# First modulation weights by columns in four parts, units 0 and 1 side by side, small vectors on the sync queue

## The reference, cut to what matters

```python
mod = (jax.nn.silu(c) @ w_ada + b_ada)[:, None, :]        # 6 x 1024 columns
sh1, sc1, gt1, sh2, sc2, gt2 = jnp.split(mod, N_MOD, axis=-1)
h = _rmsnorm(x, norm1_g) * (1.0 + sc1) + sh1
proj = h @ w_in                                            # the "units": 128 columns each
...                                                        # RWKV-7 and GLA branches, gates, merge
h2 = _rmsnorm(x, norm2_g) * (1.0 + sc2) + sh2
x = x + gt2 * _hier_moe(h2, router_group, router_expert, expert_w_gate, expert_w_up, expert_w_down)
```

## Time and profile before

| | us |
|---|---|
| time, median of 3 runs (1394.01 to 1394.71) | 1394.19 |
| profiled execution, its own time | 1392.71 |
| its span, first to last instruction | 1390.9 |
| PE busy in the span | 1329.4 (96%) |
| DVE busy | 700.9 (50%) |
| ACT busy | 491.5 (35%) |
| mean granted TensorE clock | 0.99 |

### The profile page before, as it was taken

The page is one execution under the profiler, slowest core; times in us unless marked ns, Lnnn a source line. Parts: engine busy times, 40 slices in busy tenths (PEclk is TensorE's granted clock), DMA queues, the critical chain, the costliest instruction groups (busy, mean ns, idle before and its releaser), DMA issues.

```text
span 1390.9 us, 28090 instructions
## 1 busy us (share of the span) xinstructions
PE 1329.4 (96%) x12121; PEld 987.0 (71%) x12121; DVE 700.9 (50%) x1122; ACT 491.5 (35%) x797; POOL 176.8 (13%) x216
## 2 busy tenths in 40 slices
PE   5899999999999997999999999999999999998997
PEld 1789999999999997888888998844444444433443
DVE  3423235553326665655676667725455444454454
ACT  2423235545665555555544343211000100000113
POOL 2000000000112333333433001000000000000000
PEclk9999999999999999999989999999999999999999
DMA  9557522225532220000243565999999999999993
GB/s 331 194 197 235 174 78 76 77 76 147 150 110 77 76 61 26 4 4 4 67 128 97 172 214 181 333 408 408 409 428 425 426 427 428 424 427 426 426 428 152
DMA packets 132920, 310.62 MB, mean 223 GB/s; under 512 B 13314, under 2 KB 98536, under 8 KB 119864
## 3 DMA queue, kind: packets, MB, share of 16 engines
q1 hardware_dynamic: 122078, 285.86, 54.6%
q10 hardware_dynamic: 7546, 15.58, 3.1%
q0 software_dynamic: 3168, 7.33, 1.5%
HBM read 299.88 MB, written 12.79 MB: 225 GB/s over the span
## 4 chain that ended last, share of the span: by engine, by line
PE 49%; DMA 7%; DVE 2%; ACT 1%; issue 1%; SPq 0%; DVEq 0%; ACTq 0%; POOLq 0%
PE bank L3039 13%; PE bank L2858 7%; PE bank L3063 6%; DMA lower<-in_expert_w_up 4%; PE bank L3083 4%; PE bank L2886 3%; DMA upper7b<-in_expert_w_up 2%; PE bank L1778 2%; PE bank L498 2%; PE bank L3050 1%; PE bank L3013 1%; ACT upper L1575 1%; PE bank L1844 1%; PE bank L1825 1%; PE bank L1776 1%
## 5 line engine op out<-in xcount | busy, mean ns | idle before, releaser
L953 PE MATMUL bank<-upper2end 128*128 128x272 f32 x3168 | 413.7, 291 | 5.6 <-DVE upper2end L1183 5.4
L953 PEld LDWEIGHTS bank<-upper2end 128*128 128x128 f32 x3168 | 402.1, 189 | 20.1 <-issue 19.0
L3039 PE MATMUL bank<-upper7b 128*64 128x512 f32 x784 | 230.7, 596 | 7.3 <-issue 4.2
L1160 DVE TENSOR_TENSOR upper2end<-upper,upper2end 128x1024 fp32r<-128x1024 f32 x66 | 84.8, 1284 | 250.1 <-ACT upper2end L718 249.9
L3039 PEld LDWEIGHTS bank<-upper7b 128*64 128x64 f32 x784 | 69.8, 137 | 116.5 <-issue 116.2
L3039 PE MATMUL bank<-lower,upper7b 128*64 128x512 f32 x240 | 108.6, 596 | 2.3 <-issue 1.0
L2726 ACT ACTIVATE lower<-bank 128x256 f32<-128x256 f32 x32 | 12.3, 384 | 273.6 <-PE bank L3050 273.6
L3063 PE MATMUL bank<-upper7b,lower 128*64 128x512 f32 x352 | 106.3, 595 | 0.9 <-DVE lower L3486 0.9
L3551 DVE TENSOR_TENSOR lower<-lower,bank 128x1024 f32<-128x1024 f32 (+1 forms) x70 | 82.8, 1215 | 45.4 <-PE bank L3083 42.9
L2858 PE MATMUL bank<-upper_r 128*128 128x272 f32 (+2 forms) x768 | 103.1, 293 | 0.0
L2858 PEld LDWEIGHTS bank<-upper_r 128*128 128x128 f32 x768 | 98.9, 191 | 2.9 <-issue 1.5
(11 more groups left out here) (445 smaller groups left out, 1867.4 us busy)
## 6 DMA issues: line engine op xcount, KB each, us to landing
upper7b<-in_expert_w_gate SPq DMA_DIRECT2D x20, 2048.0 KB, 23.4
upper7b<-in_expert_w_up SPq DMA_DIRECT2D x19, 2048.0 KB, 28.6
upper7b<-in_expert_w_down SPq DMA_DIRECT2D x19, 2048.0 KB, 24.3
upper<-in_w_in SPq DMA_DIRECT2D x66, 512.0 KB, 3.8
lower<-in_w_ada SPq DMA_DIRECT2D x23, 1024.0 KB, 6.9
lower<-in_expert_w_down SPq DMA_DIRECT2D x7, 2048.0 KB, 24.9
lower<-in_expert_w_gate SPq DMA_DIRECT2D x6, 2048.0 KB, 22.3
lower<-in_expert_w_up SPq DMA_DIRECT2D x6, 2048.0 KB, 28.8
```

Of the source, the lines that this page charges most:

```text
L953: m = mm(psum[s][:, c, 0:HALF], w_part[s][:, k, :], h_part[:, k, c * HALF:(c + 1) * HALF], start=k == 0 and w_part is w_high and h_part is ...
L1160: ve.tensor_tensor(w_rest[u % 2], w_slot[u % 2], w_high[u % 2].bitcast(F32), ALU.subtract).then_inc(w_split, 1)
L3039: m = nc.tensor.matmul(GU_BANK[s][64 * b:64 * b + 64, :], x_t[:, k, s * BLK:(s + 1) * BLK], w[:, k, :], start=k == 0, stop=k == KD - 1)
```

## The change

The first 2048 columns of `w_ada` are loaded in eight loads of 256 columns each, two to a part: part p holds the columns of the feature blocks 2p and 2p+1, half 0 those of `sh1` and half 1 those of `sc1`, with all 1024 rows (1 KB pieces, 1 MB a load). `x` is loaded first, in five loads with a semaphore each, then the small vectors, all by SP; then the parts, with units 0 and 1 and `xa_w` among them. ACT loads the table for the square root right after the sigmoid, with a dummy root (`root_junk`). The first modulation runs once for each part: sums, copies, columns (now a product with a stack of small identities, `id32`, that adds the four groups in the same step), bias, g1, h, split. Units 0 and 1 advance side by side, one feature block after the other, and the `xa_w` products are spread behind the blocks.

```diff
-                for k in range(KD):
-                    sp.dma_start(w_ada_1[k], w_ada_v[:, k, 0:WA]).then_inc(ada_in[k], 16)
...
+                sp.dma_start(x_tok[0:DEC, 4, :], I["x_sample"][0]).then_inc(x_in[4], 16)
+                for j in range(4):
+                    sp.dma_start(x_tok[:, j, :], I["x_prompt"][0, j * P:(j + 1) * P, :]).then_inc(x_in[j], 16)
...
+                def load_first(p, half):
+                    k0, n = PARTS[p]
+                    col = half * D + k0 * P
+                    sp.dma_start(w_first[2 * p + half], w_ada_v[:, :, col:col + n * P]).then_inc(ada_in[2 * p + half], 16)
+                for p in range(len(PARTS)):
+                    load_first(p, 0)
+                    if p == 0:
+                        load_unit(0)
+                    load_first(p, 1)
+                    if p == 0:
+                        load_unit(1)
                         sp.dma_start(xa_w, w_in_v[:, :, XA_COL:XA_COL + GATE_RANK]).then_inc(xa_in, 16)
+                for u in range(FIRST_UNITS, NU):
+                    sp.wait_ge(w_split, u - 1)
+                    load_unit(u)
+                    if u == 2:
+                        sp.wait_ge(ada_mm, 2 * len(PARTS))
...
@@ ACT @@
+                act.wait_ge(c_sig_done, 1)
+                nc.scalar.activation(root_junk, c_sig[:, 0, 0:1], ACT.Sqrt)
...
-                summed(0)
-                split(0)
-                act.wait_ge(h_smp, 2)
+                for p, (k0, n) in enumerate(PARTS):
+                    first_summed(p, 0)
+                    if p == 0:
+                        split(0)
+                    first_summed(p, 1)
+                    act.wait_ge(h_smp, 2 * p + 2)
...
@@ PE @@
+                def first_sums(p):
+                    n = PARTS[p][1] * P
+                    for half in range(2):
+                        pe.wait_ge(ada_in[2 * p + half], 16)
+                        if p == 0:
+                            pe.wait_ge(x_t_done, KD + 1)
...
+                        for k in range(KD):
+                            m = mm(bank(4 + half)[QUADS[k % 4], 0:n], c_t[:, k, :], w_first[2 * p + half][:, k, :],
+                                   start=k < 4, stop=k >= 4)
+                        m.then_inc(ada_mm, 1)
+
+                def first_columns(p):
+                    k0, n = PARTS[p]
+                    pe.wait_ge(first_copied, 2 * p + 2)
...
+                    for half in range(2):
+                        for q in range(n):
+                            at = 2 * (KD * half + k0 + q)
+                            m = mm(bank(4)[:, at:at + 2], first_parts[half][:, q * P:(q + 1) * P], id32[:, 0:2],
+                                   start=True, stop=True)
+                    m.then_inc(first_cols, 1)
...
+                def first_units(ks):
+                    for k in ks:
+                        for u in range(FIRST_UNITS):
+                            if k == 0:
+                                pe.wait_ge(w_split, u + 1)
+                                pe.wait_ge(b_t_done, 1)
+                            pe.wait_ge(h_split, k + 1)
+                            m = products(u, k)
+                            if k == KD - 1:
+                                m.then_inc(proj_mm, 1)
+                        if k == 0:
+                            pe.wait_ge(xa_in, 16)
+                        if k < KD // 2:
+                            gate_inputs(k)
+                first_sums(0)
+                first_columns(0)
+                first_units(range(0, 1))
+                first_sums(1)
+                first_columns(1)
+                first_units(range(1, 3))
+                first_sums(2)
+                first_columns(2)
+                first_units(range(3, 5))
+                first_sums(3)
+                first_columns(3)
+                first_units(range(5, KD))
+                for k in range(KD // 2, KD):
+                    m = gate_inputs(k)
+                m.then_inc(xa_mm, 1)
...
@@ DVE @@
+                def first_modulation(p):
+                    k0, n = PARTS[p]
+                    ks = slice(k0, k0 + n)
+                    v.wait_ge(first_cols, p + 1)
...
```

More of the change, by code:

```diff
@@ L208, in build @@
         boost = S2.take(T)
+        first_parts = (parts, boost[:, 0:512])
         sq = S2.take(T)
@@ L254, in build @@
         own_half = keep.take(2)
+        root_junk = keep.take(1)
         take_x, take_high = keep.take(1), keep.take(1)
@@ L720, in summed @@
                 def summed(hf):
[L721 to L737 removed]
+                    act.wait_ge(ada2_mm, 8 * hf)
@@ new lines, in summed, with first_summed @@
+                    act.wait_ge(cols_tr, hf - 1)
+                    if hf == 1:
+                        act.wait_ge(first_cols, len(PARTS))
+                    nc.scalar.activation(parts, bank((4, 7)[hf - 1]), ACT.Copy).then_inc(parts_done, 1)
+                def first_summed(p, half):
+                    n = PARTS[p][1] * P
+                    act.wait_ge(ada_mm, 2 * p + half + 1)
+                    if p:
+                        act.wait_ge(first_cols, p)
+                    nc.scalar.activation(first_parts[half][:, 0:n], bank(4 + half)[:, 0:n], ACT.Copy
+                                         ).then_inc(first_copied, 1)
@@ new lines, in _ @@
+                for p, (k0, n) in enumerate(PARTS):
[4 more added lines that the diff above has]
+                    act.wait_ge(h_smp, 2 * p + 2)
+                    for k in range(k0, k0 + n, 2):
+                        odd = h_t[:, k + 1, 0:SEQ]
+                        nc.scalar.activation(odd, odd, ACT.Identity, scale=g1[:, k + 1, 0:1], bias=mod_t[:, k + 1, 0:1]
+                                             ).then_inc(h_odd, 1)
+                        act.wait_ge(h_done, k // 2 + 1)
+                        nc.scalar.activation(h_high[:, k, :], h_t[:, k, 0:T], ACT.Copy).then_inc(h_high_done, 1)
+                        if k == 0:
+                            split(1)
+                        act.wait_ge(h_odd, k // 2 + 1)
+                        nc.scalar.activation(h_high[:, k + 1, :], h_t[:, k + 1, 0:T], ACT.Copy).then_inc(h_high_done, 1)
@@ new lines, in products @@
+                def products(u, k):
+                    for w_part, h_part in ((w_high, h_high), (w_high, h_rest), (w_rest, h_high)):
+                        for c in range(2):
+                            m = mm(psum[u % 2][:, c, 0:HALF], w_part[u % 2][:, k, :], h_part[:, k, c * HALF:(c + 1) * HALF],
+                                   start=k == 0 and w_part is w_high and h_part is h_high,
+                                   stop=k == KD - 1 and w_part is w_rest)
+                    return m
@@ L1186, in mix @@
+                split(0)
+                for p in range(len(PARTS)):
+                    first_modulation(p)
                 def mix(n, f):
```

192 lines of the change are left out of this document (88 added, 104 removed).

## The result

The changed kernel takes 1400.34 us (median of 5 runs, 1398.90 to 1401.08) against 1394.19 before (median of 5 runs, 1392.44 to 1395.30): a ratio of 1.0046, 95% interval 1.0035 to 1.0058, that is 4.9 to 8.1 us slower. The forecast was 1401.0. The profiled execution took 1399.01, its span 1397.2. Run once more on another occasion the same kernel gave 1.0032 (1.0020 to 1.0044), that is 2.8 to 6.1 us; the forecast of 6.6 lies above that second interval.

The account below looks back on a forecast made before the run. TensorE's reaching unit 2 (T) was taken to set the end: front 9.4 us sooner, round trips among the products costing more, T 64.0 against 57.36. 1394.19 + 6.6 = 1400.8, stated as 1401.0; range 1395.8 to 1406.5.

Parts of the forecast that it names:

- What bounds the kernel: TensorE up to unit 2, no slack behind the start: whatever moves PE's reaching unit 2 moves the end by as much.
- The front: Start up to unit 0's first product: x and c come sooner, first product at 30.1 instead of 39.50, 9.4 us gained.
- T: First instruction of the second modulation, when PE reaches unit 2: forecast 64.0 against 57.36; expected sign 62 to 66.
- Unit 1's block: Unit 1's first block waits for its own weights on ACT and DVE: start at 31.5, against 30.1 for unit 0.
- The rounds: Chain of block products, xa_w, sums, copy, columns and bias to product: 9.1 us each, 8.6 for block 4's.
- The clock in the rounds: PE at 1.2 GHz only for block 0, its xa_w and part of the first sums: 1.4 us, bounds 0 and 2.5.
- the clock falls in every round: Rival: idle stretches drop PE's clock in each round, about 3.8 us each; 1409; 8 in 100.
- The sum: Whole kernel: unit 2 reached 6.6 us later; 1399.3 in the profiled execution, 1400.8 on the median, stated as 1401.0.
- TensorE did not set the pace: Rival denied here: products hide the trips, T at 55.1, 1392.0; decided by PE waits under 2.2 us; 6 in 100.
- The front comes sooner and the rounds are shorter: Rival: no lower clock, shorter columns and hand-overs, 3.1 us later or below; 1396.4 with c early; 14 in 100.
- c was not late: Rival denied here: c_sample takes 6.8 us as before, everything 4.8 later, 1405.8; 7 in 100.
- The drain behind a table load: Skill's rule of 1.38 us draining on top of a table switch; would raise the forecast by 1.4; left out.

Follow-up runs that it names:

- delayed: Kernel before with 36 dummy products of 128 columns on PE just ahead of unit 2; ratio 1.0056 (1.0039 to 1.0073) to the kernel before.
- warm: Changed kernel with dummy products in three places where PE only waits; ratio 1.0024 (1.0014 to 1.0035) to the kernel before.
- sums_under_trip: Changed kernel with PE's list reordered: sums of part p+1 ahead of block 2p's products, its columns behind them; ratio 0.9993 to the kernel before.
- combined: sums_under_trip plus dummies ahead of x's transposes, DVE's small-vector copies behind x's, earlier xa_w products for blocks 4 and 5; ratio 1.0005 to before.
- small_behind: combined with small-vector loads behind the second modulation load, xa_w behind part 1, 42 dummies and x's transposes first on PE; ratio 0.9997 to before.

## Why the prediction was right, point by point

**What bounds the kernel.** That the start of unit 2 moves the end one for one agrees with delayed (8.2 us in, 7.8 out), within an interval of 5.4 to 10.2. It is not tighter than that, and the changed kernel's own loss in time (6.15 and, the second time, 4.5) is less than its 7.3 to 8.7 at unit 2; where the rest goes stays open. What I had not seen is that both ends of the ruler scatter: unit 2 of the kernel before by 1.4 us from trace to trace, the recurrences by 3.

**The front.** Forecast first product 30.1, measured 32.59 and 31.52. The step that was off is the pace of x. I let the squares run back to back (5.87 us) from 5.0; they waited 2.0 us for tiles and ended at 12.46 instead of 10.9. The transposes at the lower clock, for which I took 0.5 of at most 1, were slower than that: the first sums began at 25.13, and 22.6 was the forecast. Of these 2.5 us 1.6 are the squares and the rest, 0.9 on top of the 0.5 set down, the slow transposes; in warm, where they ran at full speed, the sums began at 23.46. So the first sign, a first product at 29 to 31.5, was missed, and so was the last square at 10 to 12; T (65.7) and the rounds lie where they were said to lie.

**Unit 1's block.** Forecast 1.4 behind unit 0's. In the changed kernel the twelve products of both are one row without a wait, 3.08 us from 32.59, because at the low clock unit 0's six take as long as unit 1's weights need. Where block 0 ran at the upper clock, PE did wait 0.37 for them and unit 1 began 1.35 (sums_under_trip) and 1.36 (warm) behind unit 0.

**The rounds.** Forecast 9.1 and 8.6, measured 9.16 and 8.72: sums 1.93 to 2.1 (1.92), copy 0.52 (0.5), columns 1.05 with the hand-over (1.05), bias to product 3.49 (3.6), a block 1.75 (1.57) and `xa_w` 0.4 to 0.6 (0.48). That these rounds are a chain made by PE's list, and not by work that has to be there, sums_under_trip shows.

**The clock in the rounds.** It fell once, ahead of block 0, and stayed up in waits of 1.35 to 1.92, as the forecast had it; the rival "the clock falls in every round" is out. The argument against it, that these waits are shorter than the 2.3 us from PE's last work to the fall, does not hold, though. PE fell idle ahead of the first product at 28.97 and 27.91 in the two traces of the changed kernel, and the clock fell at about 32.5 and at 30.0; in combined it fell at 28.0, just as PE fell idle, and in small_behind in a wait of 1.02 us. The length of a wait alone did not decide. That the rounds were spared is what the traces show; why stays open, and in the forecast it was in part luck. For block 0 and what follows it 1.4 was set down: the two traces give 0.8 and 1.8.

**The sum.** Forecast 6.6 later at unit 2. Measured 8.7 against the first trace of before and 7.3 against the second; in time 6.15 (4.9 to 8.1), and 4.5 (2.8 to 6.1) on the second occasion. From the first product to T the forecast has 33.9 us and the trace 33.1. The mechanism, an earlier front that three trips among the products more than use up, is what the runs show. That the time came out within 1 us of 1401.0 is in part luck: the front was taken 2.5 too short, and T of before (57.36) was taken from a trace that is early by 1.4 to 1.6. The two errors have opposite signs. With 58.8 for T of before the same working gives 5.2 us, 1399.4.

**The other rivals.** TensorE did not set the pace (6.15 us of waits behind the first product, the deciding point was 2.2). "The front comes sooner and the rounds are shorter" is out too: the front came later than forecast and the rounds are as long as forecast. c was not late (2.9). The weights in pieces of 1 KB were never waited for in the changed kernel; with the trips hidden and the front sooner they are (combined, small_behind). Whether that is the size of the pieces or the place in the queue was not tried. Nor does a run change the number of parts, or put units 0 and 1 one after the other again with the parts kept. The drain behind a table load (the Trainium skill, ScalarE: Activation LUTs, section What ACT_TABLE_LOAD costs) did not show here either: the dummy root starts at 4.44, 0.01 behind the end of the load at 4.43.

## What to carry to other kernels

Cutting a serial preparation into parts helps only if each part's trip across the engines lies under work that is already possible. Count the trip (here 5.1 us from the last sum to h) against what stands between its start and its first use in the in-order list, before counting instructions; here the same instructions in another order were worth 7.9 us at unit 2, and brought the time from 1.0046 or 1.0032 to 0.9993 of before. And look at what an engine does in the wait ahead of a burst: here the first twelve products behind a wait of 3.62 us took 3.08 us, and 2.0 where dummies had filled the wait.

## What the runs showed of the hardware that was not expected

The speed of PE's first work is not the same from run to run of one kernel: the same transposes took 1.09 and 1.97 us at 24.5 in two traces of the kernel before (and 1.97 in delayed), and unit 2 moved by 1.4 us. With dummy products in PE's idle start the transposes of the changed kernel took 5.9 us for 7.16 in the one trace that was taken, at no cost that could be seen.

A run's time goes with its mean granted clock. Of the 26 runs of the kernel before on one occasion the two fastest took 1388.84 and 1389.22 us at 0.993 and 0.994, and two of the slowest 1396.59 and 1396.54 at 0.987 and 0.988; the correlation over the 26 is -0.74. A difference of 0.5% between single runs of one kernel is thus nothing out of the ordinary. That the clock is the cause is not shown by this.

The fourteen small loads cost the sync queue 5.9 us of issue time (4.09 to 9.98), more than the 2.1 MB of x took it (2.3, from 1.73 to 4.05).
